# Half of the first squares on ScalarE, one weight cast earlier, and a new order of VectorE's work in the heads

## What is computed

```
mod = silu(c) @ w_ada + b_ada;  shift, scale, gate = split(mod, 3)
h = rmsnorm(x, g_norm) * (1 + scale) + shift            # needs the sum of squares of x over 2048
hq, hf, hi, mq, mk, mv, mi, mf, rq, rk, rv, z = split(h @ w_in)
for every head:                                         # chunked over the prompt, one step for the samples
    scores, state sums k^T v, outputs, new state        # ml also: normalizer n_new = decay * n + w * k
    o = head_norm(outputs) * gain (+ skip * q for ml)
o = o * silu(z)
y = x + gate * (o @ w_out)
```

## Time and profile before

| quantity | value |
|---|---|
| median of 3 runs | 2336.93 us |
| profiled execution, its time | 2337.24 us |
| its span (first to last instruction) | 2335.6 us |
| TensorE busy | 2275.7 us, 97% of the span |
| VectorE / ScalarE / GpSimd busy | 1286.6 / 738.6 / 938.5 us |
| granted TensorE clock, mean | 0.996 |
| mean DMA rate | 149 GB/s (399 and 374 GB/s in the first two of 40 slices) |

### The profile page before, as it was taken

How to read it: one execution, slowest core, us unless ns; L and a number is a source line. 1 busy time by engine, 2 the same in 40 slices (tenths; PEclk the granted TensorE clock), 3 DMA queues, 4 the chain that set the end, 5 groups by cost and what they waited for, 6 DMA issues and landing times.

```text
span 2335.6 us, 50231 instructions
## 1 busy us (share of the span) xinstructions
PE 2275.7 (97%) x21347; PEld 2164.6 (93%) x21347; DVE 1286.6 (55%) x2506; ACT 738.6 (32%) x1175; POOL 938.5 (40%) x668
## 2 busy tenths in 40 slices
PE   4899999999999999999999999999999999999998
PEld 3799999999999999998879999999999999999998
DVE  6346666677776343442137566667777753335444
ACT  2143322333333333421124333333333333334111
POOL 3043333333344343554333333333333443346552
PEclk9999999999999999999999999999999999999999
DMA  9952223544443333266775222254443323323332
GB/s 399 374 184 93 92 93 99 160 164 161 161 171 98 115 99 114 97 223 239 268 267 197 84 94 93 84 168 155 163 162 102 107 98 122 116 84 110 116 117 105
DMA packets 153648, 347.21 MB, mean 149 GB/s; under 512 B 14817, under 2 KB 85409, under 8 KB 127545
## 3 DMA queue, kind: packets, MB, share of 16 engines
q1 hardware_dynamic: 153424, 344.01, 42.8%
HBM read 312.07 MB, written 32.09 MB: 147 GB/s over the span
## 4 chain that ended last, share of the span: by engine, by line
PE 89%; DVE 4%; DMA 2%; DVEq 1%; ACT 1%; issue 1%; POOL 1%; SPq 0%; ACTq 0%; POOLq 0%
PE pj L685 72%; PE mx L691 3%; PE mx L1028 2%; PE mx L1054 2%; DMA rows<-in_ada_first 1%; PE mx L778 1%; PE mx L1042 1%; PE mx L744 1%; PE pj L1150 1%; PE mx L1006 1%; PE mx L1056 1%; DVE t L1501 1%; PE mx L1046 1%; POOL wlo L653 1%; DMA spare_piece<-in_ada_first 1%
## 5 line engine op out<-in xcount | busy, mean ns | idle before, releaser
L685 PE MATMUL pj<-hh,whi 128*128 128x260 f32 x4928 | 1417.7, 288 | 5.7 <-DVE hl L1501 5.2
L653 POOL TENSOR_TENSOR wlo<-raw,whi 128x512 fp32r<-128x512 f32 x632 | 894.6, 1447 | 1307.6 <-ACT whi L1229 1307.6
L685 PE MATMUL pj<-hl,whi 128*128 128x260 f32 x4928 | 1392.3, 283 | 0.0
L685 PE MATMUL pj<-hh,wlo 128*128 128x260 f32 x4928 | 1389.9, 282 | 0.0
L685 PEld LDWEIGHTS pj<-hh,whi 128*128 128x128 f32 x4928 | 928.0, 188 | 52.0 <-issue 45.4
L685 PEld LDWEIGHTS pj<-hl,whi 128*128 128x128 f32 x4928 | 928.4, 188 | 0.0
L685 PEld LDWEIGHTS pj<-hh,wlo 128*128 128x128 f32 x4928 | 927.9, 188 | 0.0
L1229 ACT ACTIVATE whi<-raw 128x2048 fp32r<-128x2048 f32 x158 | 302.8, 1916 | 257.4 <-PE pj L685 186.7
L1229 ACT ACTIVATE xv<-pj 128x260 f32<-128x260 f32 x188 | 64.8, 383 | 386.5 <-PE pj L685 386.2
L1501 DVE SCALAR_TENSOR_TENSOR o<-pj,mod,t 128x260 f32<-128x260 f32 (+1 forms) x56 | 24.6, 480 | 229.9 <-PE pj L685 214.3
L1229 ACT ACTIVATE t<-t 128x520 f32<-128x520 f32 (+1 forms) x126 | 79.2, 629 | 178.9 <-DVEq L1761 129.6
(11 more groups left out here) (289 smaller groups left out, 2329.8 us busy)
## 6 DMA issues: line engine op xcount, KB each, us to landing
raw<-in_w_tiles SPq DMA_DIRECT2D x128, 1024.0 KB, 4.9
raw<-in_wo_tiles SPq DMA_DIRECT2D x32, 1024.0 KB, 5.2
lev<-in_w_ada SPq DMA_DIRECT2D x90, 256.0 KB, 4.4
rows<-in_ada_first SPq DMA_DIRECT2D x22, 1024.0 KB, 20.7
lev<-in_w_ada SPq DMA_DIRECT2D x39, 512.0 KB, 5.7
out<-ss SPq DMA_DIRECT2D x32, 512.0 KB
xv<-in_w_ada SPq DMA_DIRECT2D x25, 512.0 KB, 5.8
y_kept<-o SPq DMA_DIRECT2D x2, 4160.0 KB, 18.0
```

The costliest lines, as they stand in the source:

```text
L653: last = e.tensor_tensor((wlo_third if t == 2 else wlo[:, par, :])[:, cs], w[:, cs], high_of(t)[:, cs].bitcast(F32), ALU.subtract)
L685: last = e.matmul(pj[:, 2 * par + b, 0:HALF], w[:, par, kb * P:(kb + 1) * P], x[:, kb, b * HALF:(b + 1) * HALF], start=(kb == 0 and m == 0 ...
```

## The change

At the start, ScalarE squares blocks 1, 3, ..., 13 of x into `t3` and `t4`, and VectorE only adds them. In the first head, z's weights are cast before the copies of tile 1 instead of after them, and scores and rows stand behind block 8 of the third pass instead of block 1. In all heads VectorE makes the inputs of the samples' state sums first (after `sr`), then multiplies `ss` by its decay, and in ml heads updates the normalizer only after the new `ss`. The state sums on TensorE move up by one part, in the last two ml heads of layer 1 `ml_os` as well. In the last head of a layer, two of the four `hl` subtractions move behind the new `ss`.

```
--- before.py
+++ after.py
@@ -260,7 +260,7 @@
         lb_log, lb_exp = sem("lb_log"), sem("lb_exp")
         ada_taken, ada_sum = sem("ada_taken"), sem("ada_sum")
         rs_made = sem("rs_made")
-        sq_acc, sq_sum = sem("sq_acc"), sem("sq_sum")
+        sq_acc, sq_sum, sq_odd, sq_used = sem("sq_acc"), sem("sq_sum"), sem("sq_odd"), sem("sq_used")
         h_hi, hn_ready, h_ready, hs_ready = sem("h_hi"), sem("hn_ready"), sem("h_ready"), sem("hs_ready")
         taken = sem("taken")
         out_added = sem("out_added")
@@ -327,6 +327,10 @@
         def kdec(m):
 
             return k[:, 0:T] if m == 0 else lev[:, m - 1, :]
+
+        def odd_square(kb):
+
+            return (t3, t4)[kb // 2 % 2][:]
 
         def ada_slot(piece):
 
@@ -1082,15 +1086,15 @@
                         if kind == "hg":
                             own = ({}, {2: (level_scores((-1, 0)),),
                                         **{lv + 2: (level_scores((lv,)),) for lv in range(1, 6)}},
-                                   {0: (level_scores((6,)),), 2: (rows,), 5: (states_u,), 7: (outputs,)})
+                                   {0: (level_scores((6,)),), 2: (rows,), 4: (states_u,), 7: (outputs,)})
                             return own, {5: (back,)}
                         if kind == "ml" and session_of(h, 0) >= SESSIONS[l]:
-                            return ({}, {}, {2: (scores, rows), 6: (states_u,)}), {0: (outputs,), 4: (ml_os,), 7: (back,)}
+                            return ({}, {}, {2: (scores, rows), 5: (states_u,)}), {0: (outputs,), 3: (ml_os,), 7: (back,)}
                         if kind == "ml":
-                            return ({}, {}, {1: (scores, rows), 5: (states_u,), 7: (outputs,)}), {3: (ml_os,), 7: (back,)}
+                            return ({}, {}, {1: (scores, rows), 4: (states_u,), 7: (outputs,)}), {3: (ml_os,), 7: (back,)}
                         if g == 0:
-                            return ({}, {}, {(2, 1): (scores, rows)}), {2: (states_u,), 4: (outputs,), 8: (back,)}
-                        return ({}, {}, {1: (scores, rows), 5: (states_u,), 7: (outputs,)}), {5: (back,)}
+                            return ({}, {}, {(2, 8): (scores, rows)}), {2: (states_u,), 4: (outputs,), 8: (back,)}
+                        return ({}, {}, {1: (scores, rows), 4: (states_u,), 7: (outputs,)}), {5: (back,)}
 
                 for h in range(NH):
                     kind, i, n, g, t = head_of(l, h)
@@ -1240,6 +1244,11 @@
             act(c_log, c_log, ACT.Ln, bias=1.0).then_inc(silu_log, 1)
             e.wait_ge(silu_sig, 1)
             act(c_log, c_log, ACT.Exp).then_inc(silu_exp, 1)
+            for kb in range(1, KB - 1, 2):
+                e.wait_ge(x_in[kb // 4], 16)
+                if kb > 4:
+                    e.wait_ge(sq_used, kb // 2 - 1)
+                act(odd_square(kb), o[:, kb, :], ACT.Square).then_inc(sq_odd, 1)
             def high(t, half, par, used=True):
 
                 e.wait_ge(raw_in[par], half * 16)
@@ -1356,7 +1365,7 @@
 
                             if h or j > 1:
                                 high(t + 2, (t + 2) // 2 + 1, j % 2)
-                            elif j == (0 if l else 1):
+                            elif l and j == 0:
                                 high(t0 + 3, (t0 + 3) // 2 + 1, 1)
 
                         def by_four(ap):
@@ -1406,6 +1415,9 @@
                         if kind == "rt":
                             if g:
                                 take(0, x0, PAD, swapped=t3)
+                            else:
+                                e.wait_ge(tile_done, t0 + 2)
+                                high(t0 + 3, (t0 + 3) // 2 + 1, 1)
                             take(1, x1, PAD, SCALE, swapped=t4)
                             if g == 0:
                                 take(0, x0, PAD, swapped=t3)
@@ -1542,12 +1554,24 @@
                     tt(zw[:], zw[:], z[:], A_)
                     e.drain()
 
-            for kb in range(KB):
-                if kb % 4 == 0:
-                    e.wait_ge(x_in[kb // 4], 16)
-                square(kb, kb < KB - 1)
-                if kb >= KB - 2:
-                    e.sem_inc(sq_acc, 1)
+            e.wait_ge(x_in[0], 16)
+            tt(zw[:], o[:, 0, :], o[:, 0, :], M)
+            e.drain()
+            for kb in range(1, KB - 1):
+                if kb % 2:
+                    e.wait_ge(sq_odd, kb // 2 + 1)
+                    tt(zw[:], zw[:], odd_square(kb), A_)
+                    e.drain().then_inc(sq_used, 1)
+                else:
+                    if kb % 4 == 0:
+                        e.wait_ge(x_in[kb // 4], 16)
+                    tt(z[:], o[:, kb, :], o[:, kb, :], M)
+                    e.drain()
+                    tt(zw[:], zw[:], z[:], A_)
+                    e.drain()
+            e.sem_inc(sq_acc, 1)
+            tt(z[:], o[:, KB - 1, :], o[:, KB - 1, :], M)
+            e.drain().then_inc(sq_acc, 1)
 
             for l in range(DEPTH):
 
@@ -1875,31 +1899,28 @@
 
                         if h == 3:
                             gate_diagonals()
-                        e.wait_ge(state_in[g % 2], (g // 2 + 1) * 16)
-                        tt(ss, ss, bc(token_decay, 2, HD), M)
+                        def low_first(kbs):
+
+                            for kb in kbs:
+                                e.wait_ge(o_hi, l * KB + kb + 1)
+                                tt(hl[:, kb, :], o[:, kb, :], hh[:, kb, :].bitcast(F32), S_).then_inc(o_lo_first, 1)
+
                         e.wait_ge(as_["sr"], g + 1)
                         if kind == "ml":
-
-                            ts(sw[0:GR], sr[0:GR, 1, :], gs[0:GR, i, 1:2], None, M)
-                            e.drain()
-                            e.wait_ge(nrow_in[g % 2], 32 * same_parity(g))
-                            stt(nr[0:GR], nr[0:GR], gs[0:GR, i, 0:1], sw[0:GR], M, A_)
-                            e.drain().then_inc(vs["nrow"], 1)
-                            e.tensor_tensor_reduce(out=t3[0:GR, 0:HD], in0=nr[0:GR], in1=sr[0:GR, 0, :], scale=1.0, scalar=0.0,
-                                                   op0=M, op1=A_, accum_out=sm[0:GR, 63:64])
                             ts(sw[0:GR], sr[0:GR, 2, :], gs[0:GR, i, 1:2], None, M)
                             e.memset(vt[:, :, HD:HD + 1], 1.0)
                             blocks(sr[0:GR, 1, :], big[0:GR, 0:256])
-                            blocks(sr[0:GR, 0, :], q_pairs[0:GR, :])
                         else:
                             blocks(sr[0:GR, 2, :], big[0:GR, 0:256])
                         e.drain().then_inc(vs["blk"], 1)
-
+                        e.wait_ge(state_in[g % 2], (g // 2 + 1) * 16)
+                        tt(ss, ss, bc(token_decay, 2, HD), M)
+                        if kind == "ml":
+                            blocks(sr[0:GR, 0, :], q_pairs[0:GR, :])
+                        e.drain()
 
                         if h + 1 == NH:
-                            for kb in range(LOW_FIRST):
-                                e.wait_ge(o_hi, l * KB + kb + 1)
-                                tt(hl[:, kb, :], o[:, kb, :], hh[:, kb, :].bitcast(F32), S_).then_inc(o_lo_first, 1)
+                            low_first(range(LOW_FIRST // 2))
                         e.wait_ge(ps["u"], g + 1)
                         e.wait_ge(stored, 16 * stores_before(g))
                         w = HD + 1 if kind == "ml" else HD
@@ -1915,6 +1936,18 @@
                         ss4 = ss.rearrange("p (j s) v -> p j (s v)", s=2)
                         tt(ss4, ss4, mx[:, 0:4, 256:512], A_)
                         e.drain().then_inc(vs["ss"], 1)
+                        if kind == "ml":
+                            kn = t3[0:GR, HD:2 * HD]
+                            ts(kn, sr[0:GR, 1, :], gs[0:GR, i, 1:2], None, M)
+                            e.drain()
+                            e.wait_ge(nrow_in[g % 2], 32 * same_parity(g))
+                            stt(nr[0:GR], nr[0:GR], gs[0:GR, i, 0:1], kn, M, A_)
+                            e.drain().then_inc(vs["nrow"], 1)
+                            e.tensor_tensor_reduce(out=t3[0:GR, 0:HD], in0=nr[0:GR], in1=sr[0:GR, 0, :], scale=1.0, scalar=0.0,
+                                                   op0=M, op1=A_, accum_out=sm[0:GR, 63:64])
+                            e.drain()
+                        if h + 1 == NH:
+                            low_first(range(LOW_FIRST // 2, LOW_FIRST))
 
 
                         e.wait_ge(ps["o"], g + 1)
```

## The result

The changed kernel took 2323.66 us (median of 4 runs, 2323.1 to 2328.12) beside 2337.01 us (2336.76 to 2337.56) of the kernel before: a ratio of 0.9945, 95% interval 0.9932 to 0.9957, so 13.4 us less. The forecast was 2323.1 us. The profiled execution took 2323.1 us, its span 2321.5 us. In `kernel.py` the lines of TensorE, ScalarE and GpSimd are now 4 further down (`back` L695, `states_u` L1046, `outputs` L1058), and those of VectorE's helpers 12 (L1507, L1510, L1513).

A forecast was written before the change was run, and what follows sets the result against it. TensorE is busy nearly the whole span, so only its waits can be won. Terms 9.3 + 2.9 + 2.3 - 0.3 - 0.4 = 13.8 us off 2337.24 gave 2323.4, median 2323.1 us; range 2319.6 to 2328.6 us.

The forecast's parts named there:

- Outputs: All heads: state sums one part earlier remove TensorE's waits for VectorE at `outputs`; 9.3 us gained, upper end 11.0.
- no waits: Rival: the short waits at `outputs` are only the cost of taking a semaphore, 5.4 us stay, 2328.5 us; chance 0.06.
- VectorE not free: Rival: VectorE is busy when the state sums land, chains start as before, 9.3 us stay, 2332.4 us; chance 0.05.
- nothing moves: Rival: the waits reappear at `states_u`, within 0.2% of before, 2334 us or so; chance 0.02.
- `blk`: Three ml heads: blocks came late behind the normalizer, which now stands behind `ss`; 3 x 0.95, 2.9 us gained.
- `ml_os`: Last two ml heads of layer 1: moved one part earlier, it removes two waits of `back`; 2.3 us gained.
- Last heads: TensorE reaches the second output tile 1.3 us sooner, GpSimd's subtractions keep their time; 0.3 us lost over two layers (0 to 2.5).
- z's cast: First head: VectorE's rotation of k starts 1.9 us later, delaying scores; 0.4 us lost (gain 0.4 to loss 1.3).
- all seven: First head: all seven VectorE operations of k's rotation slowed beside GpSimd, making the loss 1.3 us.
- Squares: Start: seven products leave VectorE's chain, but transfers hide it and `norm` has nothing to gain; 0 us.
- The head norm's slower rival: Rival: GpSimd's subtraction slows more of VectorE's head norm, `back` late; 2329 or 2347 us; chance 0.04.

The follow-up runs named there:

- order: Kernel before with VectorE's new order in the heads alone; TensorE's hooks, the start and the first head as before: 2333.22 us, ratio 0.9981.
- hooks: Kernel before with only TensorE's hooks moved (states_u one part earlier in all heads but the first, ml_os too), VectorE's order old: 2345.78 us, ratio 1.0033.
- latecast: Changed kernel with ScalarE's last three casts of o (blocks 12 to 14) issued after VectorE's output of the last head: 2321.89 us, ratio 0.9932.
- nocast: Changed kernel with the first head's cast of z's weights behind the copies again and the scores' hook back in block 1: 2324.63 us, ratio 0.9939.
- nosq: Changed kernel with all squares of x back on VectorE: 2323.74 us, ratio 0.9942.
- sqonly: Kernel before with ScalarE's squares of x alone: 2336.55 us, ratio 0.9993.
- pad: Kernel before with eight tiny single-column writes ahead of VectorE's squares, making its program longer: 2335.9 us, run once.
- a0: The changed kernel again, unaltered, timed beside the kernel before: 2322.72 us, ratio 0.9938.
- lowfour: Changed kernel with all four of VectorE's subtractions ahead of the chain of the last heads, as before: 2328.76 us, ratio 0.9953.
- a1: The changed kernel once more, unaltered, on a second occasion beside the kernel before: 2323.73 us, ratio 0.9940.

## Why the prediction came out right

The total was right to 0.6 us, and the mechanism of the main terms too. That it was right so closely is luck: two terms were mis-sized by about 2 us each, and their errors cancel.

- **Outputs, forecast 9.3 us: 11.8 us.** By starts the 32 waits summed to 9.5 us and sum to 0.2 now, as forecast. What I left out stands in the earlier trace rows: behind a wait the first four matmuls take 0.71 us, without one 0.61. A plain head whose wait was 0.20 us is 0.28 us shorter as a whole, so 31 x 0.08 us come on top: 9.3 + 2.5. I had taken the 11.0 us of the weight loads as the upper end, and the truth lies above it. The rival "no waits" is refuted by order and the changed kernel together; "VectorE not free" by 1.3 us of margin; "nothing moves" by `states_u` without a wait.
- **`blk`, forecast 2.9 us: 3.1 us.** 2.85 us by starts, and 0.07 us per wait in the matmuls behind (1.13 against 1.06 us). VectorE's order did it: order has it, hooks does not.
- **`ml_os`, forecast 2.3 us: 2.4 us.** 1.04 and 1.22 us by starts and 0.06 each behind. This one is the hook's: gone in hooks, there in order.
- **Last heads, forecast 0.3 us back: 2.2 us.** The direction was right and the size was not. The prediction says that TensorE gets there 1.3 us sooner "while GpSimd's subtractions for it start at the old time", and that is what the timelines show: 11.3 us behind `outputs` in place of 10.0. What I priced at 0.15 us per layer has two parts. TensorE waits 0.51 us by starts for `wlo`, where it waited for nothing before. And the subtractions, late against VectorE's work, now lie on the fifth scaling, 1.33 us in place of 0.33, so that `back` waits 0.93 us and not 0.37. Together they are 1.07 of the 1.09 us by which F is longer. latecast keeps the wait for `wlo` (0.49 us) and takes all the overlap away, the one on the four other scalings too, which the kernel before already had (4.92 us against 2.88); there 1.03 us per layer come back. The range of 0 to 2.5 held it. The Trainium skill (SBUF — State Buffer, Who interferes with whom) says that `tensor_scalar` can take the ports shared with GpSimd, and that whoever comes second waits for the whole instruction; 1.33 against 0.34 us agrees. I had applied that section to the first head alone.
- **z's cast, forecast 0.4 us of loss: 0.1 us.** nocast against the changed kernel, 23.03 and 23.14 us. In both some of VectorE's operations are slowed to 1.6 to 1.8 us and some are not, so "all seven" was too many; in the changed kernel it was five.
- **Squares, forecast 0 us: 0 us as to their work**, by nosq and sqonly. But their code moved VectorE's program, and that brought 0.3 to 0.4 us in B. What they do to A is within its spread: 120.42 to 123.20 us in five profiles without them, 121.01 to 124.02 in nine with them.
- **The head norm's slower rival** didn't come: no wait of `back` in any middle head.

The placement was a term that I didn't have. VectorE's instruction that adds to `ss` stood idle 0.52 us in one head of the kernel before, 0.17 in pad, where nothing about it differs:

```profile
776.66 1.22 DVE L1495 TENSOR_TENSOR ss<-ss,mx 128x1024 f32<-128x1024 f32 x1 [0.52 <-issue]
```

```profile
776.26 1.22 DVE L1495 TENSOR_TENSOR ss<-ss,mx 128x1024 f32<-128x1024 f32 x1 [0.17 <-issue]
```

Two of the three waits of 0.54 us that I counted follow from such a start of the addition to `ss`, the third from 0.43 us of idle time ahead of an instruction on `st`; in pad, sqonly and order all three are 0.2 us. From `by_pass` on pad takes 1.4 us less than before and sqonly 1.6. Of the 15.2 us that the changed kernel gains there, though, only the 0.4 us in B can be put down to it: hooks has two of these late starts still (0.54 and 0.52 us) and no wait of `outputs` in their heads, so the earlier state sums cover them anyway. The terms sum to 11.8 + 3.1 + 2.4 - 2.2 - 0.1 + 0.4 = 15.4 us, against 15.2 us in this profile and 14.8 us in a0. In the one head where a wait for `blk` and one behind `ml_os` both fell (outputs 55.80 us apart before, 53.78 us now) they gave 1.7 us together and not 2.1. A ran 1.0 us against it in the profile.

## What to carry to other kernels

A wait of 0.2 us in each of 32 heads is worth removing, and it costs more than its idle time (0.28 us here): count also how much longer the instructions behind it take than where there is no wait. Move the consumer's input and the producer's order together; VectorE's order alone gave 4.4 us, the hooks alone cost 7.7 us, and both with the start's edits gave 13.4 us. One part more lost 10 of these, because every margin must also hold the handing over (0.13 to 0.26 us here). When a stall goes, the engines that did not wait for it keep their time: list what they now do at the same moment, above all the two that share ports. Here 1.1 of the 1.3 to 1.4 us gained in each last head were lost again, half to such an overlap and half to weights that were not ready, and issuing three casts 7.5 us later brought 1.03 us back there. Then look at the whole kernel: 0.5 us was lost again at a place that the edit doesn't touch.

## What the hardware showed unexpectedly

- A wait of TensorE can be paid twice. Between 112 us and the last microseconds of the span the lower clock shows in these profiles only at or close behind a long wait: at the place of the last point here, and in four of the five places with 2.18 to 2.40 us of idle time (both last heads of lowfour, two of three ml heads of hooks), where the granted clock fell to 0.50 and, with part of the stretch at full clock, 0.56 and 0.54. Behind waits of 1.6 us and less it was 1.00 in all fourteen profiles (and the row at 547.30 above).
- VectorE's delay in taking up an instruction depends on the place of its program: 0.13 or 0.51 us at one instruction, 0.17 or 0.52 us at another, alike in each profile of one kernel. That the fetching of instructions is behind it wasn't tried.
- The same wait does not bring the lower clock each time. Ahead of layer 1's first tile TensorE stood idle for 1.85 to 1.87 us in all 14 profiles, and 6 of them ran the next microseconds at the lower clock, which cost 1.3 us in a1, whatever the kernel was.
